# Gated recurrence of the third block: picks two levels behind, ends, output and state update later in a head

## The reference

```python
def hgrn2_direction(q, log_f, k, v):
    """S_t = diag(f_t) S_{t-1} + k_t v_t^T, o_t = S_t^T q_t."""
    def step(state, inp):
        qc, gc, kc, vc = inp
        cum = jnp.cumsum(gc, axis=1)
        seg = cum[:, :, None] - cum[:, None, :]
        decay = masked_decay(seg, tri)
        attn = jnp.einsum("bthk,btshk,bshk->btsh", qc, decay, kc)
        y_intra = jnp.einsum("btsh,bshv->bthv", attn, vc)
        y_inter = jnp.einsum("bthk,bhkv->bthv", qc * jnp.exp(cum), state)
        cum_end = cum[:, -1]
        new_state = (jnp.exp(cum_end)[..., None] * state
                     + jnp.einsum("bshk,bshv->bhkv", kc * jnp.exp(cum_end[:, None] - cum), vc))
        return new_state, y_intra + y_inter
```

## Time and profile before

| | us |
|---|---|
| median of 3 runs | 4512.72 (4509.75 to 4515.1) |
| the profiled execution | 4505.31 |
| its span | 4503.5 |
| busy: PE, DVE, ACT, POOL | 3737.5, 1381.8, 698.2, 225.3 |

### The profile page before, as it was taken

The page is one execution under the profiler, slowest core; times in us unless marked ns, Lnnn a source line. Parts: engine busy times, 40 slices in busy tenths (PEclk is TensorE's granted clock), DMA queues, the critical chain, the costliest instruction groups (busy, mean ns, idle before and its releaser), DMA issues. The chain is left out here.

```text
span 4503.5 us, 32149 instructions
## 1 busy us (share of the span) xinstructions
PE 3737.5 (83%) x11618; PEld 1804.1 (40%) x11618; DVE 1381.8 (31%) x2445; ACT 698.2 (16%) x1295; POOL 225.3 (5%) x241
## 2 busy tenths in 40 slices
PE   6976667799878499999999997694699667589998
PEld 2524233344343144444444443243344556334444
DVE  0015422239221411211112112327533577511011
ACT  1021110101110210100001000312252233110000
POOL 0000000210000100000000001000000444000000
PEclk8985557899999699999999998896799888899999
DMA  2211631462110599999999996112222000212221
GB/s 77 68 58 50 228 130 43 144 226 82 56 48 19 230 365 403 400 409 400 400 407 401 409 400 220 56 38 72 83 75 75 5 5 1 75 56 75 75 75 37
DMA packets 219296, 729.49 MB, mean 162 GB/s; under 512 B 16208, under 2 KB 27105, under 8 KB 184375
## 3 DMA queue, kind: packets, MB, share of 16 engines
q1 hardware_dynamic: 179132, 629.94, 37.0%
q10 hardware_dynamic: 28394, 55.66, 3.5%
q0 software_dynamic: 11664, 42.47, 2.7%
HBM read 678.33 MB, written 49.69 MB: 162 GB/s over the span
## 5 line engine op out<-in xcount | busy, mean ns | idle before, releaser
L1623 PE MATMUL bank<-moe_gu,all_hT 128*128 128x512 f32 x1088 | 471.9, 594 | 0.0
L1117 PE MATMUL bank<-all_hT,early_w 128*128 128x512 f32 x896 | 390.0, 598 | 22.6 <-PEq L135 11.7
L1813 DVE TENSOR_TENSOR all_hT<-bank,moe_bias 128x512 f32<-128x512 f32 x51 | 35.3, 692 | 971.9 <-PE bank L1623 682.4
L1623 PEld LDWEIGHTS bank<-moe_gu,all_hT 128*128 128x128 f32 x1088 | 207.5, 191 | 261.1 <-issue 261.1
L1649 PE MATMUL bank<-moe_dn,moe_rows 128*128 128x512 f32 x544 | 265.7, 651 | 44.6 <-DMA moe_dn<-in_w_dn_dram 43.7
L1117 PEld LDWEIGHTS bank<-all_hT,early_w 128*128 128x128 f32 x896 | 171.9, 192 | 240.7 <-issue 240.7
L1636 PE MATMUL bank<-moe_gu,all_hT 128*64 128x512 f32 x1088 | 236.5, 592 | 1.0 <-issue 1.0
L2590 PE MATMUL bank<-hg_qs,hg_ks 128*128 128x128 f32 x896 | 138.3, 302 | 115.6 <-DVE hg_ks L2562 113.8
L1117 PE MATMUL bank<-all_hT,late_w 128*128 128x512 f32 x512 | 221.9, 596 | 12.1 <-PEq L135 12.1
L2334 PE MATMUL bank<-all_hT,hin_w 128*128 128x512 f32 x512 | 222.7, 598 | 9.9 <-PEq L372 9.9
L1117 PE MATMUL bank<-b_up,late_w 128*128 128x512 f32 x512 | 220.0, 592 | 1.7 <-PEq L1089 1.7
(11 more groups left out here) (533 smaller groups left out, 4095.6 us busy)
## 6 DMA issues: line engine op xcount, KB each, us to landing
moe_gu<-in_w_gu_dram SPq DMA_DIRECT2D x136, 2048.0 KB, 21.1
moe_dn<-in_w_dn_dram SPq DMA_DIRECT2D x68, 2048.0 KB, 22.9
early_w<-in_w_in_dram SPq DMA_DIRECT2D x13, 2048.0 KB, 9.0
expert_rows<-conv_zeros POOLq DMA_DIRECT2D x49, 512.0 KB, 17.2
early_w<-in_w_mod_dram SPq DMA_DIRECT2D x12, 2048.0 KB, 8.1
early_w<-in_ada_w_dram SPq DMA_DIRECT2D x12, 2048.0 KB, 7.9
hin_w<-in_w_in_dram SPq DMA_DIRECT2D x10, 2048.0 KB, 8.4
late_w<-in_w_up_dram SPq DMA_DIRECT2D x8, 2048.0 KB, 9.0
```

The lines of the kernel that those rows point to most:

```text
L1117: mm = nc.tensor.matmul(B[b][:], w[:, k, m * P:(m + 1) * P], src[:, i * KT + k if stacked else k, :], start=(k == 0), stop=(k == KT - 1))
L1623: mm = nc.tensor.matmul(B[bank][:], xb2[:, k, :], gu[:, q, kk, col:col + HALF], start=(k == 0), stop=(k == KT - 1))
L1813: after(vec.tensor_tensor(g, gate[:], bias[0], ALU.add), 1)
```

## The change

It reorders the work of a head on four engines. Nothing is added or removed.

- VectorE: the scaling of the next head's level 0 stands ahead of pick 5 of the current head, and picks 6 and 7 behind it. A pick follows its level's scaling by two levels instead of one. The end multiplies stand behind level 1, `finish` behind pick 1 (between levels 3 and 4), the state updates behind level 6 and pick 4.
- TensorE: the output of head h - 1 goes behind level 1, the transposes behind level 2, U behind level 4.
- GpSimd and ScalarE: the end subtract and the end exponentials stand ahead of level 2 instead of ahead of level 0; `turned_out` stands behind level 4 instead of level 2.

```diff
@@ gpsimd
+            def end_diff(h):
+                ...
+            for h in range(HG_H):
                 for i, m in enumerate(LEVELS):
                     n = h * NL + i
+                    if i == 2:
+                        end_diff(h)
@@ scalar
+            for h in range(HG_H):
                 for i, m in enumerate(LEVELS):
                     n = h * NL + i
+                    if i == 2:
+                        ends(h)
...
-                    if i == 2:
+                    if i == 4:
                         turned_out(h)
@@ vector
-                pick(h, NL - 1)
-                pick(h, NL)
+            scale(0, 0)
+            for h in range(HG_H):
+                if h:
+                    pick(h - 1, NL - 1)
+                    pick(h - 1, NL)
+                scale(h, 1)
+                scale_ends(h)
+                scale(h, 2)
+                pick(h, 0)
+                scale(h, 3)
+                pick(h, 1)
+                if h:
+                    finish(h - 1)
+                scale(h, 4)
+                pick(h, 2)
+                scale(h, 5)
+                pick(h, 3)
+                scale(h, 6)
+                pick(h, 4)
+                states(h)
+                if h + 1 < HG_H:
+                    scale(h + 1, 0)
+                pick(h, 5)
+            pick(HG_H - 1, NL - 1)
+            pick(HG_H - 1, NL)
             finish(HG_H - 1)
@@ tensor
                     pairs(h, i, qs[:, n % R, :], ks[:, n % R, :])
-                    if i == 0:
+                    if i == 1 and h:
+                        output(h - 1)
+                    if i == 2:
                         pe.wait_ge(end_scaled, h + 1)
...
-                        if h:
-                            output(h - 1)
-                    if i == 3:
+                    if i == 4:
                         pe.wait_ge(turned_copied, h + 1)
```

More of the change, by code:

```diff
@@ L2477, in _ @@
             nc.gpsimd.memset(S[:, order[0], :], 0.0).then_inc(zeroed, 1)
-            for h in range(HG_H):
+            def end_diff(h):
                 g = G[:, h, :].rearrange("p (c t) -> p c t", t=P)
+                e = (kd if d == 0 else qe)[:, h % 2, :].rearrange("p (c t) -> p c t", t=P)
                 if h >= 2:
                     pool.wait_ge(end_scaled, h - 1)
-                e = (kd if d == 0 else qe)[:, h % 2, :].rearrange("p (c t) -> p c t", t=P)
-                if h >= 2:
                     pool.wait_ge(out_made, h - 1)
@@ L2505, in turned_out, with ends @@
                 nc.scalar.copy(kdT[:], B[4][:]).then_inc(turned_copied, 1)
-            for h in range(HG_H):
+            def ends(h):
                 act.wait_ge(end_diffed, h + 1)
@@ L2551, in finish, with scale, scale_ends @@
                     vec.tensor_tensor(y[:, h, :], y[:, h, :], B[6 + h % 2][:], ALU.add).then_inc(added, 1)
-            for h in range(HG_H):
+            def scale(h, i):
+                m = LEVELS[i]
+                n = h * NL + i
+                dve.wait_ge(exped, n + 1)
+                qd, qq, kk, kq = (halves(x, m) for x in (qs[:, n % R, :], q[:, h, :], ks[:, n % R, :], kh[:, h, :]))
+                vec.tensor_tensor(qd[:, :, q_half, :], qd[:, :, q_half, :], qq[:, :, q_half, :], ALU.mult)
+                vec.tensor_tensor(kk[:, :, k_half, :], kk[:, :, k_half, :], kq[:, :, k_half, :],
+                                  ALU.mult).then_inc(scaled, 1)
+            def scale_ends(h):
                 dve.wait_ge(end_exped, h + 1)
@@ L2556, in _ @@
                 vec.tensor_tensor(kd[:, h % 2, :], kd[:, h % 2, :], kh[:, h, :], ALU.mult).then_inc(end_scaled, 1)
[L2557 to L2577, removed]
@@ L2578, in _, with states @@
-                pick(h, NL - 1)
-                pick(h, NL)
+            def states(h):
+                for j, c in enumerate(order[:-1]):
+                    dve.wait_ge(u_made, h + 1)
+                    if h or j:
+                        dve.wait_ge(state, (TT - 1) * h + j)
+                    if h and j == 0:
+                        dve.wait_ge(out_made, h)
+                    vec.scalar_tensor_tensor(out=S[:, order[j + 1], :], in0=S[:, c, :],
+                                             scalar=dec[:, h, c:c + 1], in1=B[5][:, c * P:(c + 1) * P],
+                                             op0=ALU.mult, op1=ALU.add).then_inc(state, 1)
```

## The result

The changed kernel takes 4479.23 us in the median (4473.07 to 4480.58, 4 runs) against 4511.24 (4509.06 to 4515.1) of the kernel before on the same chip. The ratio is 0.9925 with a 95% interval of 0.9908 to 0.9943, a gain between 25.7 and 41.5 us. The profiled execution took 4478.22 with a span of 4476.4, 27.1 less than the 4503.5 of before.

What follows compares the result with a forecast made beforehand. VectorE and TensorE waiting for each other by turns was taken to bound the recurrence; gains of 17.65 (six heads at 17.5, last 14.2, first 0.7) and 18 us, together 36, take the 4512.7 median to 4476.5, range 4460 to 4498.

Steps and rivals of the forecast that it cites:

- recorded gain of 28 to 46: Whole kernel: gain in us set beside heads of 17.0 to 18.35 us, given a chance of 0.62.
- the sign of being right: Recurrence heads: 2.0 us less from pick 6 of one head to pick 6 of the next.
- the ends: First and last heads of a direction: pick 6 of the first 0.7 us earlier, last head 14.2 us.
- waits for TensorE (2.95 us a head): VectorE's idle ahead of pick 0, output copy and pick 6 (0.58, 1.49, 0.61, plus drained pipeline) all goes at full clock.
- other signs: No wait ahead of the output copy, no idle at picks, half multiplies no shorter in mean than 602 ns.
- Collisions with GpSimd: VectorE multiplies against GpSimd subtracts: 2.44 us a head becomes 3.89; with 13.16 of bare work, 17.05 a head.
- the layout: One head laid out by steps: subtracts meet multiplies of levels 1, 3, 5, 6 (+0.86, +0.59, +1.25, +1.19 us).
- The clock: one head in three loses 1.3: TensorE at half clock behind the boundary gap: one head in three grows from 17.05 to 18.35 us, taken as 17.5.
- Rival (c): ScalarE's queue, copy ahead of level 5 exponentials, eats the gain: 19.4 us a head, 4505; chance 0.08, shared with another rival.
- (d): TensorE's clock never returns to full inside a head: 22.5 us a head, 4544; chance 0.06 including other losses.
- Second direction 18 us: Second direction of the recurrence: same instructions, stretch 1.0 us shorter, so a gain of 18 us, together 36.
- (a): GpSimd's row of subtracts costs double: collisions about 6, 19.2 us a head, 4499; sign, half multiplies above 750 ns; chance 0.12.

Runs made afterwards that it cites:

- e1_warm: Changed kernel plus 8 unused identity products between the next head's products of levels 0 and 1, where TensorE idles: stage 293.29 us, ratio 0.9920 to before.
- e6_small_sub: e1_warm with GpSimd's level subtracts done for 128 of 512 columns only (another result): stage 246.43 us, heads of 13.93 us.
- e8_gated: Changed kernel, subtracts released by VectorE's scaling three levels back, pick 7 behind level 1, end subtract and exponentials ahead of level 3: 4429.94 us, 0.9821 of before.
- e5_after_again: Changed kernel run once more without any edit: stage 310.02 us, ratio 0.9926 to the kernel before.

## Why the prediction was right, point by point

Forecast 4476.5, measured 4479.2; forecast gain 36, measured 32.0 in the medians and 27.1 between the two profiled executions. That the time came within 3 us is in part luck. The sum was made for the stage, and there the change gave 25.9 us instead of 35.7: 7.3 instead of 17.65 in the first direction, 18.6 instead of 18 in the second. The profiled execution of before lies 5.9 us below its median, that of the changed kernel 1.0, and this covers half of the miss. The recorded gain of 28 to 46 doesn't follow from the 17.0 to 18.35 a head beside it either: by the prediction's own sum these give 41 to 25, and the stage came out at the low end.

The direction and the mechanism held: waits for products went, collisions with GpSimd grew. By parts, from pick 6 of head 0 to pick 6 of head 7 the two directions take 8.8 and 20.3 us less (forecast 16.95 each), 2.08 a head on average where 2.0 was given as the sign of being right; and the ends cost 3.2 us where 1.4 were to be gained.

- **VectorE and TensorE waited by turns; the waits for TensorE (2.95 us a head) go at full clock.** Right where the clock allows: in the second direction VectorE waits for TensorE 1.8 us in all ahead of the first seven additions, and ahead of no pick. In the first direction the wait ahead of the copy, which was to be gone, is 0.6 or 1.7 us in each head. Of the changed kernel's other signs, picks have no idle, but the first halves of the multiplies have a shorter mean than before (553 against 602 ns); the longer partners (786 and 770 against 537 and 521) carry the collisions.
- **Collisions with GpSimd grow from 2.44 to 3.89 a head, the head takes 17.05.** 3.96 and 16.98 in the second direction, 16.90 in e1_warm. The places differ from the layout (an end multiply and level 2 in place of levels 1 and 3, levels 5 and 6 as laid out), the sum does not; that it agrees to 0.1 with half of its places wrong is luck. e6_small_sub shows the mechanism: shorter subtracts, shorter heads. The rule cited from the Trainium skill ("SBUF — State Buffer", "SBUF: two separate sides") stands with this: the shortest steady head with full subtracts is e8_gated's 14.96, and none went below the 14.2 estimated with it.
- **The clock: one head in three loses 1.3.** This term was mis-sized. In the first direction all six heads lost, 1.3 and 2.4 by turns, mean 18.79 against 17.5: 7.7 us. The last output of that direction ran at half clock too (its copy waited 3.77 us, 2.14 before): 1.6 more. Together with the first head (0.7 forecast; its picks stand as in the earlier trace rows, pick 6 at 27.50 us from the start of the stage instead of 27.58) and the last (14.6 against 14.2) that is the difference of the first direction, 7.3 us instead of 17.65. I had taken the low stretches as chance, spread over heads; e5_after_again repeats them as a fixed pattern of the loop.
- **Rival (c)'s path was real.** The wait of 0.60 for ScalarE's exponentials of level 5, behind the copy of kdT behind the slow output, stands in each head of the first direction. I gave 0.6 us in hand and 1.6 to a half-clock output, which says that it would bite; I counted it in the 1.3 and not in how often.
- **In (d): busier in the mean, so less half-clock time than before.** Wrong: the granted clock fell from 0.88 to 0.83 and 0.85, the time at 1.2 GHz rose from 81.9 to 99.0 us. TensorE did the same products in less time, but spread more evenly, in groups of 0.9 us with gaps. That this spread is the reason is argued; no run varied it alone. The Trainium skill's sentence ("TensorE: Matmul & The Clock Gate", "Part 1: The HAM clock gate") speaks of recent busy-ness; a mean over a head, as I used it, is not that. e1_warm agrees with the sentence: products put into the gap raised the granted clock to 0.93 and 0.92.
- **Second direction 18 us.** 18.6 measured, by two misses that cancel: from pick 6 of head 0 to that of head 7 it gains 20.3, since five heads take 16.97 and the heads of before were 19.6 in the mean; its first head takes 1.8 us more (pick 6 at 27.43 us from the start of the direction instead of 25.67) where 0.7 less was laid out.
- **Rival (d)** didn't come: the lowest mean clock of a head is 0.76, at the start of the second direction (18.75 us). Neither did (a): multiplies in the row of subtracts waited for one subtract, not for two, and the mean of a half multiply is 665 ns over both halves (its sign was 750).

What was left out is that parts of the change work against one another, by way of the clock and of the collisions: three of its moves, each taken back alone, gave a shorter stage. That was nowhere in the prediction.

## What to carry to other kernels

Lay one round of the loop out with steps from start to start, including what excludes what; it gave the head to 0.1 us here, where the clock left it alone, and for e8_gated (12.9 and 2.0 against 14.96), though not the places of the collisions. When the waits between two engines are gone, look for the exclusion between VectorE and GpSimd, and release GpSimd's instruction by the VectorE instruction ahead of one that reads PSUM (a pick, a copy), so that the two run side by side: one changed wait took 33 us off the stage here, half of it by way of the clock. Before a reordering is called good as a whole, take its moves back one at a time: here less of it was worth more. And see on which of TensorE's instructions the stretches at 1.2 GHz fall in each round: on a result that is waited for they cost full price, and a small shift of order, or work that nobody needs in the gap, moves or removes them.

## What the runs showed of the hardware that I had not expected

- The clock's low stretches can come at the same place of a loop in every round: one pattern of six heads (18.3, 19.3 by turns) in one direction, another (16.97, the low stretch where nobody waits) in the other, both repeated in a second execution to 0.05 us.
- Adding 16 matmul records a head, 1.8 us of TensorE's work, shortened a head from 18.8 to 16.9, and in the kernel before the stage by 15.3 us.
- A masked copy with its mask in SBUF and its data in PSUM, and a state update with one operand in PSUM, run beside GpSimd's subtract at their full pace (a pick 0.74 with the subtract, 0.72 without; three state updates 1.24 either way), while a multiply of two SBUF operands stretches from 0.42 to up to 1.31 until the subtract is through.
